# A hybrid pooling and state-space block: transposes of x ahead of the row sums, and a third product among the first two

## The reference

```python
mod = jax.nn.silu(c) @ w_ada + b_ada
shift, scale, gate = jnp.split(mod, 3, axis=-1)
h = rmsnorm(x, norm_pre) * (1.0 + scale[:, None, :]) + shift[:, None, :]
proj = h @ w_in
u_pool, z_pool, u_ssm, z_ssm, g_pool, g_ssm = jnp.split(proj, list(IN_SPLITS), axis=-1)
y_pool = causal_pool_mixer(u_pool, pool_w, pool_scale) * jax.nn.silu(z_pool)
y_ssm = s5_mixer(u_ssm, ...) * jax.nn.silu(z_ssm)
merged = (jax.nn.sigmoid(g_pool) * (y_pool @ w_branch_pool)
          + jax.nn.sigmoid(g_ssm) * (y_ssm @ w_branch_ssm))
out = merged @ w_out
return x + gate[:, None, :] * rmsnorm(out, norm_post)
```

## Time and profile before

| | |
|---|---|
| time, median of 3 runs | 981.72 us (980.82 to 982.67) |
| the profiled execution | 980.43 us, span 978.3 us |
| PE busy | 946.9 us, 97% |
| DVE busy | 650.5 us, 66% |
| ACT busy | 344.4 us, 35% |
| POOL busy | 47.1 us, 5% |

### The profile page before, as it was taken

The page is one execution under the profiler, slowest core; times in us unless marked ns, Lnnn a source line. Parts: engine busy times, 40 slices in busy tenths (PEclk is TensorE's granted clock), DMA queues, the critical chain, the costliest instruction groups (busy, mean ns, idle before and its releaser), DMA issues.

```text
span 978.3 us, 11720 instructions
## 1 busy us (share of the span) xinstructions
PE 946.9 (97%) x4512; PEld 794.6 (81%) x4512; DVE 650.5 (66%) x912; ACT 344.4 (35%) x384; POOL 47.1 (5%) x82
## 2 busy tenths in 40 slices
PE   0999999999999999999999999999999999999997
PEld 0878888888888888888888888888888888787886
DVE  6968978988888858768877667663345444455233
ACT  6532341322343334543645445631122221133111
POOL 0019700000000000000000000000000000000000
PEclk9999999999999999999999999999999999999999
DMA  9733273444445477765757553897543345322222
GB/s 342 291 119 98 92 269 138 173 152 151 151 152 185 176 222 199 238 186 174 203 160 224 158 163 87 270 341 254 179 151 107 108 191 218 129 86 87 86 86 86
DMA packets 95687, 168.28 MB, mean 172 GB/s; under 512 B 37648, under 2 KB 54160, under 8 KB 95632
## 3 DMA queue, kind: packets, MB, share of 16 engines
q1 hardware_dynamic: 86272, 163.07, 49.9%
q10 hardware_dynamic: 9360, 4.46, 2.1%
HBM read 118.21 MB, written 49.28 MB: 171 GB/s over the span
## 4 chain that ended last, share of the span: by engine, by line
PE 91%; DVE 5%; ACT 2%; DMA 1%; issue 1%; SPq 0%; ACTq 0%; DVEq 0%
PE ps L1784 51%; PE ps L1873 17%; PE ps L1973 8%; PE psb L1873 4%; PE ps L1919 2%; PE psb L1842 1%; PE psa L1894 1%; PE psa L1784 1%; PE psb L1908 1%; PE psb L1906 1%; DMA sin_t<-yp_d 1%; PE psa L1837 1%; PE psb L1808 1%; DVE mod_out L1261 0%; ACT gt L977 0%
## 5 line engine op out<-in xcount | busy, mean ns | idle before, releaser
L1784 PE MATMUL ps<-bop,w_hi 128*128 128x512 f32 x1312 | 352.7, 391 | 0.4 <-DVE bop L1295 0.3
L1784 PEld LDWEIGHTS ps<-bop,w_hi 128*128 128x128 f32 x1312 | 245.2, 188 | 51.6 <-DVE bop L1295 0.5
L1784 PE MATMUL ps<-bop,w_lo 128*128 128x512 f32 x656 | 201.9, 389 | 0.0
L1784 PEld LDWEIGHTS ps<-bop,w_lo 128*128 128x128 f32 x656 | 123.2, 188 | 25.6
L1257 DVE TENSOR_TENSOR w_lo<-raw,w_hi 128x1024 fp32r<-128x1024 f32 x49 | 61.4, 1255 | 59.9 <-ACT w_hi L965 59.8
L965 ACT ACTIVATE w_hi<-raw 128x1024 fp32r<-128x1024 f32 x49 | 51.6, 1057 | 95.1 <-PE ps L1784 87.7
L1873 PE MATMUL ps<-bop,r_hi 128*128 128x512 f32 x208 | 64.1, 389 | 0.0
L1873 PE MATMUL ps<-t_hi,r_hi 128*128 128x512 f32 x140 | 55.1, 394 | 0.0
L1873 PE MATMUL ps<-t_hi,r_lo 128*128 128x512 f32 x140 | 54.6, 390 | 0.0
L1873 PE MATMUL ps<-t_lo,r_hi 128*128 128x512 f32 x140 | 54.5, 389 | 0.0
L1973 PE MATMUL ps<-wo_hi,y_hi 128*128 128x512 f32 x128 | 49.9, 390 | 0.4 <-DVE wo_lo L1714 0.4
(11 more groups left out here) (301 smaller groups left out, 1533.6 us busy)
## 6 DMA issues: line engine op xcount, KB each, us to landing
raw<-in_wstream SPq DMA_DIRECT2D x58, 512.0 KB, 5.1
pair_raw<-in_wstream SPq DMA_DIRECT2D x22, 512.0 KB, 4.8
ada<-in_w_ada SPq DMA_DIRECT2D x16, 512.0 KB, 12.2
x_tok<-in_x SPq DMA_DIRECT2D x8, 512.0 KB, 6.8
gs_d<-gt SPq DMA_DIRECT2D x8, 512.0 KB, 5.1
win_d<-win_new SPq DMA_DIRECT2D x8, 512.0 KB, 4.4
wout_d<-wout_new SPq DMA_DIRECT2D x8, 512.0 KB, 5.7
wout<-wout_d SPq DMA_DIRECT2D x8, 512.0 KB, 4.8
```

Source lines behind the costliest of these rows:

```text
L1784: last = mm(ps[slot(u)][:, f * HALF:f * HALF + HALF], a[:, k, :], b(k, f), start=k == 0 and q == 0, stop=k == KT - 1 and q == 2)
```

## The change

It touches the first part of the program alone, up to the coefficients. The order of loads: `cols`, then the x tiles, with the state-space parameters behind tile 2, c behind tile 3 and `consts` behind tile 4; the first two weight tiles go behind the first and the second pair of `ada` loads. Of the 8 sums of squares, DVE makes two (tiles 2 and 5), ACT six. The transposes have four PSUM pairs: channel blocks 0 to 3 are transposed for tokens 0 to 511 as soon as their four `diag` matrices are there, then for the rest. From block 2 on ACT first copies the PSUM pair out into `h_full[k]` (`xt_out`), and makes h in place later (`h_of`). The third product, `gs` 2, runs its k steps among the last ones of `gs` 0 and 1. On DVE `reduced_angles` and `sine` move from before the row sums to behind the last `split_h`, and `split_lo(3)` to before `cos_sin`.

```diff
-        xt = [psa, psb]
+
+        xt = [ps[0], ps[1]] + [psb, psa] * 3
...
+            sp.dma_start(cols[:, :], cols_d).then_inc(cols_in, 16)
             for t in range(CH):
                 sp.dma_start(x_tok[:, t, :], x_view[t]).then_inc(tile_in[t], 16)
-            load_w(0)
-            load_w(1)
+                if t == 2:
+                    sp.dma_start(par["are"], a_re_d).then_inc(par_in, 16)
+                    sp.dma_start(par["aim"], a_im_d).then_inc(par_in, 16)
+                    sp.dma_start(par["ldt"], log_dt_d).then_inc(par_in, 16)
+                if t == 3:
+                    sp.dma_start(silu_row[:, :], c_d).then_inc(c_in, 16)
+                if t == 4:
+                    sp.dma_start(consts[:, :], consts_d).then_inc(small_in, 16)
             for k in range(KT):
+                if k in (1, 2):
+                    load_w(k - 1)
...
+            def xt_out(k):
+
                 act.wait_ge(xt_done, k + 1)
+                fn(h_full[k][:, :], xt[k][:, :], ACT.Copy).then_inc(xt_taken, 1)
...
+            split_hi(0)
+            h_of(0)
+            h_high(0)
+            xt_out(2)
+            split_hi(1)
+            h_of(1)
+            xt_out(3)
+            h_high(1)
+            for k in range(2, KT):
+                if k + 2 < KT:
+                    xt_out(k + 2)
+                if k == 6:
+                    split_hi(2)
+                h_of(k)
+                h_high(k)
...
+            def square_sum(t):
+                dve.wait_ge(tile_in[t], 16)
+                stt(rt[1][:, :], x_tok[:, t, :], 1.0, x_tok[:, t, :], ALU.mult, ALU.mult,
+                    accum_out=stat[:, 0, t:t + 1]).then_inc(v_sums, 1)
...
+                if half_ == 0:
+                    dve.wait_ge(par_in, 16 * 3)
+                    plain_angles(steps)
...
                 scale_shift(k)
                 if k:
                     split_h(k - 1)
+                if k < 2:
+                    split_lo(k)
+                if k == 6:
+                    split_lo(2)
             split_h(KT - 1)
-            split_lo(2)
+            reduced_angles(steps)
+            sine(steps)
+            split_lo(3)
             cos_sin(steps)
-            split_lo(3)
+            split_lo(4)
             magnitudes(steps)
             dve.wait_ge(angle_ready, 1)
             factors(steps)
-            split_lo(4)
             complex_factor(steps)
...
+            for tiles in (range(0, 4), range(4, CH)):
+                for k in range(4):
+                    transposed(k, tiles)
+            third = {5: (0, 1), 6: (2, 3), 7: (4, 5, 6, 7)}
             for k in range(KT):
...
+                step(0, k)
+                step(1, k)
+                for k3 in third.get(k, ()):
+                    step(2, k3)
+                if k + 4 < KT:
+                    transposed(k + 4, range(CH))
+            for u in FIRST[3:]:
                 product(u, h)
```

More of the change, by code:

```diff
@@ L81 @@
 JOB = {u: j for j, u in enumerate(JOBS)}
+X_TILES_ACT, X_TILES_DVE = ((0, 1, 3), (4, 6, 7)), ((2,), (5,))
 SLOT = [j if j < 3 else (j - 1) % 2 for j in range(len(JOBS))]
@@ L962, in split_hi @@
                 act.wait_ge(raw_in[p % 2], 16 * (p // 2) + 16)
-                if previous(p) is not None:
+                if p == 2:
+                    act.wait_ge(xt_done, KT)
+                elif previous(p) is not None:
                     act.wait_ge(mm_done, previous(p) + 1)
                 fn((wx_hi if p == 2 else w_hi[p % 2])[:, :, :], raw[p % 2][:, :, :], ACT.Copy).then_inc(hi_done, 1)
[L967 to L973, removed]
-                    act.wait_ge(tile_in[t], 16)
-                    if t:
-                        act.wait_ge(x_sums, t)
-                    fn(gt[t % 2][:, :], x_tok[:, t, :], ACT.Square, accum_out=stat[:, 0, t:t + 1]).then_inc(x_sums, 1)
+            act.wait_ge(cols_in, 16)
+            fn(stat[:, 5, 0:1], cols[:, 0:1], ACT.Silu)
+            done = 0
+            for half_, tiles in enumerate(X_TILES_ACT):
+                for t in tiles:
+                    act.wait_ge(tile_in[t], 16)
+                    if done:
+                        act.wait_ge(x_sums, done)
+                    fn(gt[done % 2][:, :], x_tok[:, t, :], ACT.Square, accum_out=stat[:, 0, t:t + 1]).then_inc(x_sums, 1)
+                    done += 1
+                if half_ == 0:
+                    act.wait_ge(c_in, 16)
+                    fn(silu_row[:, :], silu_row[:, :], ACT.Silu).then_inc(silu_ready, 1)
                 act.wait_ge(x_var, half_ + 1)
@@ L1261, in row_sum @@
                 return stt(scratch_, row, 1.0, halves(silu_row[:, :]), ALU.mult, ALU.mult, accum_out=acc)
-            dve.wait_ge(small_in, 16 * 5)
-            plain_angles(steps)
-            reduced_angles(steps)
+            def square_sum(t):
+                dve.wait_ge(tile_in[t], 16)
+                stt(rt[1][:, :], x_tok[:, t, :], 1.0, x_tok[:, t, :], ALU.mult, ALU.mult,
+                    accum_out=stat[:, 0, t:t + 1]).then_inc(v_sums, 1)
             for half_ in range(2):
                 cols4 = slice(4 * half_, 4 * half_ + 4)
-                dve.wait_ge(x_sums, 4 * half_ + 4)
+                for t in X_TILES_DVE[half_]:
+                    if half_:
+                        dve.wait_ge(v_sums, half_)
+                    square_sum(t)
+                if half_ == 0:
+                    dve.wait_ge(par_in, 16 * 3)
+                    plain_angles(steps)
+                dve.wait_ge(v_sums, half_ + 1)
+                dve.wait_ge(x_sums, 3 * half_ + 3)
                 ts(stat[:, 1, cols4], stat[:, 0, cols4], 1.0 / D, EPS, ALU.mult, ALU.add).then_inc(x_var, 1)
@@ L1272, in _ @@
                 newton(steps, cols4, 1.0)
+                dve.wait_ge(small_in, 16)
                 for t in range(4 * half_, 4 * half_ + 4):
@@ L1275, in _ @@
                 if half_ == 0:
[L1276 to L1281, removed]
+                    dve.wait_ge(silu_ready, 1)
+                    dve.wait_ge(cols_in, 16)
+                    do(ts(g_col[:, :], b_ada[:, KT:2 * KT], 1.0, None, ALU.add))
             def scale_shift(k):
@@ L1801, in product, with transposed, step @@
                 last.then_inc(mm_done, 1)
[L1803 to L1808, removed]
-                              start=True, stop=True)
[L1810 to L1816, removed]
-            for k in range(KT):
[L1818 to L1825, removed]
+            def transposed(k, tiles):
+                if k >= 4:
+                    pe.wait_ge(xt_taken, k - 3)
+                for t in tiles:
+                    if k == 0:
+                        pe.wait_ge(x_scaled, t + 1)
+                    last = mm(xt[k][:, t * P:t * P + P], x_tok[:, t, k * P:k * P + P], diag[:, t, :],
+                              start=True, stop=True)
+                if CH - 1 in tiles:
+                    last.then_inc(xt_done, 1)
+            def step(n, k):
+                u = ("gs", n)
+                if k == 0:
+                    begin(u)
+                    if n == 1:
+                        pe.wait_ge(h_ready, 2)
+                    elif n == 2:
+                        pe.wait_ge(xt_taken, KT - 2)
+                pe.wait_ge(h_done, k + 1)
+                last = k_step(u, k, *h)
+                if k == KT - 1:
+                    last.then_inc(mm_done, 1)
+            for tiles in (range(0, 4), range(4, CH)):
+                for k in range(4):
+                    transposed(k, tiles)
+            third = {5: (0, 1), 6: (2, 3), 7: (4, 5, 6, 7)}
+            for k in range(KT):
+                step(0, k)
[5 more added lines that the diff above has]
+            for u in FIRST[3:]:
                 product(u, h)
```

24 lines of the change are left out of this document (12 added, 12 removed).

## The result

The changed kernel is slower: 984.84 us (median of 8 runs, 982.11 to 986.04) against 980.92 (8 runs, 980.05 to 982.67) for the kernel before, a ratio of 1.0037 with a 95% interval of 1.0025 to 1.0049. That is 3.9 us more. The forecast was a gain of 0.7 us and a time of 981.0; the measured time is 1.6 us above the upper end of my range.

A forecast was written before the change was run, and what follows sets the result against it. PE bounds the kernel (busy 946.9 of 978.3 us). Its 5.3 us lead meets the chain over `cos_sin` and POOL: pairs at 139.15 instead of 139.88, so 981.72 - 0.7 = 981.0 us, range 978.6 to 983.2 (8 in 10).

The forecast's parts named there:

- a wait of 1.51 before k = 5: PE's first k loop: PE would wait 1.8 us there, for block 7's transposes, copy, h and split.
- the wait for the fourth tile: DVE would be ready at 64 and wait for the tile's high part, covering up to 6.4 us of moved work.
- The waits for low parts: PE would wait for tiles 6 and 9 in DVE's queue; some 4.5 us in all between 90 and 140.
- the gain of PE's lead: PE would be 5.3 us ahead at the third product's end; only 0.7 us would remain at the pairs.
- rival (b): Clock falls to 1.2 GHz between transposes and products, at 23.5; price 1.8 us or more, 982.8 or 985.5; chance 10%.
- these waits lie in front of the later one and don't add to it: PE's waits for low parts before the pairs would add nothing to the last wait; pairs at 139.15.
- Terms of the chain that were too small: Second chain: `cos_sin` would end at 72.65, then 66.5 us to the pair's first low part, at 139.15.
- the 1 us that I gave either way and took at zero: POOL's 78 instructions beside a denser DVE: 49.8 us as before, with 1 us allowed either way.
- One reading in the prediction: Behind the first product: two transposed blocks less than before, 3.5 us, within PE's lead.
- the 1.8 us of the rows: Slow first passes after idle, 3.78 - 1.95; left out of the sum, with it +1.1 us (slower) instead of -0.7.

The follow-up runs named there:

- run 4: Kernel before, with reduced_angles and sine made once more and cos_sin put behind split_lo(3), so that its second chain is late; 984.44 us, ratio 1.0036.
- run 2: Changed kernel plus twelve repeated transposes of block 3, keeping TensorE busy between 23.8 and 27.5 us; 985.14 us, ratio 1.0040.
- Run 3: Changed kernel plus fourteen products into an unused bank ahead of `zs` 0, filling the second idle stretch; 983.82 us, ratio 1.0032.
- run 1: Changed kernel with one line moved: cos_sin ahead of split_lo(3), the low part of tile 3; 985.66 us, ratio 1.0040.
- run 5: Changed kernel with the low parts of weight tiles 5, 7 and 8 earlier in VectorE's queue, cos_sin left in place; 985.28 us, ratio 1.0048.
- run 6: Changed kernel with both edits: cos_sin ahead of split_lo(3), and low parts of tiles 5, 7 and 8 earlier; 980.84 us, ratio 0.9999.
- run 8: Kernel before with the low parts of tiles 5, 7 and 8 moved earlier and nothing else, as a control; 980.26 us, ratio 0.9999.
- run 9: Run 7's kernel with the first pair's two low parts ahead of the last t_lo in VectorE's order; 983.00 us, ratio 1.0021.
- run 7: Changed kernel with cos_sin first, low parts of tiles 5, 7 and 8 early, and twelve repeated transposes of block 3; 979.54 us, ratio 0.9989.

## Why the prediction was wrong

*What held.* PE's front: transposes from 15.01 (I had 14.5), first product at 27.49 (27.2), a wait of 1.51 before k = 5 (1.8). `reduced_angles` and `sine` are covered by the wait for the fourth tile, as I said: VectorE stood idle 3.29 us behind them. The waits for low parts came where I had them, at the sixth and the ninth tile (tiles 5 and 8), 1.37 + 3.44 = 4.8 us between 90 and 140 where I had 4.5, the wait at the pairs included. And the gain of PE's lead is not kept, because the chain over `cos_sin` and GpSimd sets the earliest start of the pairs: run 4 shows that chain alone in the old kernel.

*What failed.* The forecast had the pairs at 139.15; in the profile they start at 145.09, 5.9 us later. Three parts, each with its row:

- *The clock left out of the sum*, which I had as rival (b) with 10%: the granted clock fell in the idle stretch behind the transposes. Its price, put at 1.8, was 4.41 - 2.72 = 1.7 us on block 0. In the sum here all of it goes through to `cos_sin`; that it did is argued, since in run 2, with the clock up, only part of what block 0 was early arrived there.
- *"these waits lie in front of the later one and don't add to it"*. This is the step that failed. I saw that PE would wait for low parts on the way, and took a wait for lost time only. I had all of them end ahead of a last wait at the first half product; in the trace PE has no wait there. The wait before `zs` 0 brought the low clock, and 2.9 us of slow work (13.84 for 10.90) are not in front of anything: at full clock PE would have come at 142.2 and waited until 142.9; it came at 145.09. 2.2 us. Run 3 shows it: with the stretch filled, `zs` 0 starts when it did and the pairs 1.9 us earlier.
- *Terms of the chain that were too small*, 2.0 us: the first product 0.3 late, GpSimd 50.8 us instead of 49.8 (the 1 us that I gave either way and took at zero), and 0.7 more between block 0 and the end of `cos_sin`, which I can't pin to one row.

One reading in the prediction is also wrong, without weight for the forecast: behind the first product there is one transposed block less than before (four for five, 1.8 us), not two (3.5 us).

1.7 + 2.2 + 2.0 = 5.9. Without the clock, the pairs would stand at 145.09 - 3.9 = 141.2, 1.3 us later than before, not 0.7 earlier. One run of the changed kernel had a mean granted clock of 0.999, as the kernel before has; it took 982.11 us, 1.2 over before. The other seven, at 0.993 to 0.997, took 984.1 to 986.04. So about 1.2 us of the loss of 3.9 would belong to the order of the work, and about 2.7 to the clock, in part directly and in part through the chain that it makes later. That split rests on one run and on the sum of one profile; it is argued, not shown. It doesn't contradict run 4, whose chain was made late by hand, by as much as order and clock together made it late here.

*What I had not seen* is that two bounds stood side by side. VectorE works without a break from 69 to 131 us and feeds both: the chain (what it does first) and PE's weight tiles (what it does in between). Moving one forward moved the other back: run 1 took 7 us off GpSimd's end and gave 3.7 of idle at tile 5, the work ahead of its low part having taken 4 us longer; run 5 took away the wait before `zs` 0 and gave 4.4 before the pairs; only run 6 took both. In the order of before PE came later and VectorE started earlier, and all low parts were in time by themselves (run 8).

The Trainium skill's page TensorE: Matmul & The Clock Gate, Part 1, which I had cited and not used, has TensorE fall back to half its clock when idle. The changed kernel and runs 1, 2, 3, 5 and 9 agree, with the numbers above; run 6, with 3.24 us of idle and a granted clock of 1.00 behind it, doesn't show it. With the 1.8 us of the rows in the sum, the forecast would have been +1.1 us: the right sign, and a third of the size.

*What stays open*: why the low clock comes behind one idle stretch and not behind another of nearly the same length (3.15 and 3.24 us); what makes VectorE's and GpSimd's work longer in one order than in another; and whether the remaining wait of 1.8 us at the pairs could be had, with ScalarE's order changed too.

## What to carry to other kernels

A head start of the bounding engine is worth only what every feeder behind it can follow, so list for each later tile who makes it, when, and what stands ahead of it in that engine's queue; here two such bounds lay 2.2 us apart (145.09 and 142.9), and runs 1 and 5, which removed one each, showed no gain. And an idle stretch of a busy TensorE has two prices, the stretch itself and the slow work behind it: in run 9 one wait of 3.15 us cost more than the short ones of run 7, and in runs 3 and 7 work that is thrown away was a filling that paid (1.0 and 1.3 us in the medians). So a wait that "lies in front of a later one" is not free for that reason alone: look at the granted clock behind it.

## What the runs showed of the hardware

In the profiled executions of all eleven kernels, between 15 and 200 us, TensorE stood idle 36 times for 0.26 to 1.80 us behind busy work, and its granted clock fell behind none. There were ten longer stretches, and it fell behind nine; in brackets the granted clock of the windows of 5 us that it touched:

- 2.73 us (0.69 and 0.63; run 1) and 3.71 us (0.86, 0.50, 0.96; run 1)
- 3.15 us (0.84, 0.82; run 9)
- 3.35 us (0.91, 0.75; run 5) and 4.44 us (0.68, 0.64; run 5)
- 3.44 us (0.55, 0.77) and 3.73 us (0.81, 0.85), both in the changed kernel
- 3.44 us (0.51, 0.80; run 2)
- 3.95 us (0.79, 0.87; run 3)
- 3.24 us, with 1.00 throughout: the one without a fall (run 6)

A fall cost 1.7 and 2.9 us where durations could be compared. The mean granted clock of a whole execution was 0.992 to 0.998 with a fall in the profile and 0.998 or 0.999 without one. I had not expected idle times of about 3 us, in a kernel whose TensorE is busy for 97% of the span, to decide the outcome.

GpSimd's same 78 instructions took 49.8 to 50.9 us in the kernel before, the changed one and runs 2 to 5, and 46.2 to 47.0 us in runs 1 and 6 to 9. VectorE worked beside them in all, in different orders.
